# The second feed-forward layer of token block B as seven quarter products instead of eight, in a float32 decoder layer on one core

## The chip, the cores and the metric

One Trainium2 chip, one of its cores. The metric is the device time of one execution of the whole program in microseconds. Engines: TensorE (PE, with its weight loads as PEld), VectorE (DVE), ScalarE (ACT), GpSimd (POOL), SyncE (SP, which here only issues DMAs).

## What is computed

One hybrid decoder layer in float32: 1024 prompt tokens and 8 sample tokens, width 1024. Only its last third matters here:

```python
x = x + jnp.einsum('bte,ed->btd', mix, p['w_out'])        # 1024 x 1024
h2 = rmsnorm(x, p['norm_ffn_g'])
u = jnp.square(jax.nn.relu(jnp.einsum('btd,df->btf', h2, p['w_up'])))   # 1024 -> 4096
x = x + jnp.einsum('btf,fd->btd', u, p['w_down'])         # 4096 -> 1024
```

The outputs are the rows x of all tokens, and keys, values and recurrent states of the attention part, which comes earlier.

## The kernel before

**Numbers.** Each operand of a dense product is split in two parts of the type fp32r, a high one (a copy in that type, made by ScalarE) and a low one (value minus high, made by VectorE). A product of two tiles is three matmuls: high by high, high by low, low by high (`split_matmuls`, lines 85, 86 and 87, which serve all dense products). The stationary operand is a 128x128 piece of the weights, the moving one a piece of the tokens' data.

**Blocks.** The tokens are worked on in two blocks: A has prompt tokens 0 to 511, B has the other 512 and the 8 sample tokens, in two spans of 256 and 264 columns. The program goes through a front part (all tokens' projections), then `feed_forward` for A, with attention and recurrences of both blocks woven between its steps, then `feed_forward` for B with nothing beside it. Block B's part is what the change touches.

**Feed-forward of B.** The order on TensorE is: eight tiles "out" (`w_out`, 8 tiles x 2 spans x 24 matmuls), and then eight groups g. A group has four tiles "up" x = 0 to 3 (128 of the 4096 inner features each: 2 spans x 8 inputs x 3 = 48 matmuls a tile) and one "down" part: the group's 512 inner features into the 1024 outputs, that is 8 output tiles o x 2 spans x 4 inputs x 3 = 192 matmuls. Each of the 16 sums of a down part takes one PSUM bank in turn out of four, and VectorE adds it to the rows `xt` (line 2254). The output is kept transposed in `xt`, and at the end TensorE turns it tile by tile (`turn_y`, line 2045), ScalarE copies it (`copy_y`, line 2113) and SP stores it. Two of the four turns of prompt tokens stand inside the last down part, and there are two buffers `y`.

**Beside TensorE**, each engine has its instructions in an order written out by hand, and executes them in that order. In each up tile of B:

- ScalarE: high part of 128 rows of `w_down` (line 2095, 128x1024), high part of the up weights two tiles ahead (`split_high`, line 2080, 128x1024), for each span the square (line 2153) and the high part of the result (line 2155). It also issues the loads of `w_down` (line 2102).
- VectorE: low part of the `w_down` rows (line 2190, 128x1024), for each span relu and scaling out of PSUM (line 2236), low part of the up weights two tiles ahead (`split_low`, line 2084, 128x1024), for each span the low part of the squares (line 2243). In the down part it has the 16 adds.
- GpSimd: in the out tiles the sum of squares for the norm (line 2179), one `pow` for it (line 2184), and nothing in the groups.
- SP: loads of up weights, three tiles ahead.

Group 0 has the norm in it. TensorE sums the squares after tile 0 (line 1975), VectorE scales them (line 2195), GpSimd takes the root (line 2184), VectorE makes five small diagonal pieces (line 2200), and in the middle of tile 1's second span TensorE spreads these over the partitions (line 1982). ScalarE copies the result (line 2145), and only then can the first relu run.

What orders the engines are semaphores. `take` makes TensorE wait until the bank's former owner was read:

```python
    def take(pe, kind, *key):
        i = place[kind, key]
        if i >= BANKS:
            pe.wait_ge(*freed(i - BANKS))
```

Of the kernel before, what the change touches and what calls it, by code (L numbers as in the profile page):

```python
# [15 lines left out]
P = 128  # L16
# [3 lines left out]
NS = 8  # L20
# [60 lines left out]
def split_matmuls(pe, out, lhs, rhs, ks, first, last):  # L81

    for n, k in enumerate(ks):
        (lh, ll), (rh, rl) = lhs(k), rhs(k)
        pe.matmul(out, lh, rh, start=first and n == 0, stop=False)  # L85
        pe.matmul(out, lh, rl, start=False, stop=False)  # L86
        ins = pe.matmul(out, ll, rh, start=False, stop=last and n == len(ks) - 1)  # L87
    return ins
# [1678 lines left out]
def feed_forward(nc, a, m, ps, sem, at, part):  # L1767
    spans = [(0, HALF)] if part == 0 else [(0, 256), (256, 264)]
    NP = len(spans)
    N = HALF + part * NS  # L1770
    BANKS = 2 + 2 * part
    sfx = "AB"[part]
    mh, ml = m["mh"][part], m["ml"][part]
    xt, xr, rb2 = m["xt"], m["xr"], m["rb2"]
    x2h = at("x2h" + sfx, (59.5, 166.625)[part], [P, KT, NB], FP32R)
    x2l = at("x2l" + sfx, (75.75, 182.875)[part], [P, KT, NB], FP32R)
# [14 lines left out]
    if part:  # L1791
        norm_tiles.append((slice(N - P, N), slice(HALF, N)))
# [4 lines left out]


    OUT0, UP0, DOWN0 = KT * part, FT * FGROUPS * part, KT * FGROUPS * part

    def out_no(u, p):
        return OUT0 + NP * u + p

    def up_no(g, x, p):
        return UP0 + NP * (FT * g + x) + p

    def down_order(g):
        if part and g == FGROUPS - 1:
            return [(o, p) for p in range(NP) for o in range(KT)]
        return [(o, p) for o in range(KT) for p in range(NP)]  # L1810

    def down_no(g, o, p):
        return DOWN0 + NP * KT * g + down_order(g).index((o, p))


    order = [("out", (u, p)) for u in range(KT) for p in range(NP)]
    for g in range(FGROUPS):
        order += [("up", (g, x, p)) for x in range(FT) for p in range(NP)]
        order += [("down", (g, o, p)) for o, p in down_order(g)]
    place = {what: i for i, what in enumerate(order)}  # L1820

    def freed(i):
        kind, key = order[i]
        if kind == "out":
            return x2_made, out_no(*key) + 1
        if kind == "up":
            return v_made, up_no(*key) + 1
        return added, down_no(*key) + 1

    def norm_bank(p):  # L1830
        return 7 - p if part else 6
# [4 lines left out]
    def take(pe, kind, *key):  # L1836
# [3 lines left out]
        elif part == 0:  # L1840
            m["dense_bank_free"](pe, i)
        elif i < 2:
            pe.wait_ge(added, DOWN0)
        else:
            m["side_banks_free"](pe)

    def tile_no(t):
        return TILES * part + t

    def tile_done(t):  # L1850

        if t >= KT:
            g, x = divmod(t - KT, FT)
            return up_ready, up_no(g, x, NP - 1) + 1
        if t >= 0:
            return out_ready, out_no(t, NP - 1) + 1
        return up_ready, UP0 + t + 1

    def tokens(p):
        return slice(spans[p][0], spans[p][0] + spans[p][1])  # L1860

    ALL = slice(0, N)

    def sync(sp, beside):
        def load_up(t):
            if part or t >= 2:
                sp.wait_ge(up_low, tile_no(t) - 1)
            else:
                sp.wait_ge(sem("w_low"), 22 + t)
# [11 lines left out]
        def load_residual(u):  # L1881
            if u >= 2:
                sp.wait_ge(x2_made, out_no(u - 2, NP - 1) + 1)
            elif part:
                sp.wait_ge(u_low, UP0)
            else:
                m["residual_stored"](sp)
            sp.dma_start(xr[:, u % 2, 0:N], a["xt_scratch"].rearrange("p (k n) -> p k n", n=NT)
                         [:, u, part * HALF:part * HALF + N]).then_inc(xr_in[u % 2], 16)

        def store_y(t):

            n = 4 * part + t
            sp.wait_ge(y_copied, n + 1)
            if t == 4:
                sp.dma_start(a["y_sample"], m["y"][0:NS, t % 2, :]).then_inc(sem(f"y_out{t % 2}"), 16)
            else:
                sp.dma_start(a["y_prompt"][(4 * part + t) * P:(4 * part + t + 1) * P, :], m["y"][:, t % 2, :])\
                    .then_inc(sem(f"y_out{t % 2}"), 16)

        if part == 0:
            load_up(2)
        for t in range(KT):
            load_residual(t)
            load_up(t + 3)
            if t >= KT - 2 and part == 0:
                first_down(t - KT + 2)
            if part and t in (0, 2):
                m["store_yA"](t)
                m["store_yA"](t + 1)  # L1910
# [3 lines left out]
        for g in range(FGROUPS):  # L1914
            for x in range(FT):
                t = KT + FT * g + x
                if t + 3 < TILES or part == 0:
                    load_up(t + 3)
# [6 lines left out]
        m["store_y" + sfx] = store_y  # L1925
# [7 lines left out]
    def tensor(pe, beside):  # L1933
# [3 lines left out]
        def out_part(u, p, ks):  # L1937
            if ks[0] == 0:
                pe.wait_ge(up_low, tile_no(u) + 1)
                take(pe, "out", u, p)  # L1940
            ins = split_matmuls(pe, ps[:, bank("out", u, p), 0:spans[p][1]], weights(u),
                                lambda k: (mh[:, k, tokens(p)], ml[:, k, tokens(p)]), ks, ks[0] == 0, ks[-1] == KT - 1)
# [3 lines left out]
        def first_outs():  # L1946

            for i in range(2):
                pe.wait_ge(sem("mix_low"), 8 if i else 4)
                for u in range(2):  # L1950
                    out_part(u, 0, range(4 * i, 4 * i + 4))
                    beside(2 * i + u)

        def first_out():

            for p in range(NP):
# [1070 lines left out]
```

## Time and profile before

| | us |
|---|---|
| time, median of 3 runs | 1424.47 (1423.86 to 1426.74) |
| span of the profiled execution, first to last instruction | 1424.1 |
| TensorE busy | 1375.1 (97% of the span) |
| VectorE busy | 834.5 (59%) |
| ScalarE busy | 542.6 (38%) |
| GpSimd busy | 318.1 (22%) |
| start of B's first up tile | about 1041.5 |
| one group of B | 46.0 |
| last matmul of B's last down part | 1415.0 |

The profiled execution's span is its own time but for what lies outside its instructions. It stands 0.4 below the median of the runs and inside their range. Start times in all rows count from the first instruction of the span. "Busy" of an engine is the union of its instructions. In a timeline row "x2" means two instructions after each other shown as one, and "idle" names what ended the wait.

### The profile page before, as it was taken

The page shows a single profiled execution, that of the slowest core. Times are in us where ns is not written, and L with a number is a line of the kernel's source. Part 1 is how long each engine was busy: PE and PEld are TensorE (multiplying, and loading weights), DVE is VectorE, ACT ScalarE, POOL GpSimd, SP SyncE. Part 2 cuts the span into 40 slices and gives each one's busy share as a digit, 9 for nine tenths or more (in the row PEclk, how much of TensorE's full clock was granted, in tenths as well). Part 3 has the DMA queues.
Part 4 walks back from the last instruction along what each step waited for, and adds up shares of the span by engine and source line. Part 5 has one row for each costly group of instructions (what it writes and reads, how often), then busy time and mean ns, then how long its engine had stood idle before and what let it go on. Part 6 is the DMA issues. An engine that isn't in the chain of part 4 may idle for free.

```text
span 1424.1 us, 23612 instructions
## 1 busy us (share of the span) xinstructions
PE 1375.1 (97%) x8781; PEld 1145.8 (80%) x8781; DVE 834.5 (59%) x1416; ACT 542.6 (38%) x1011; POOL 318.1 (22%) x363
## 2 busy tenths in 40 slices
PE   7998999999999999998999999999999999999998
PEld 6767777776777767776767767667999999999998
DVE  5469667745648886758667564444454455445542
ACT  6444332414546554533325241332442234223431
POOL 2546624435523534342000000000220000000000
PEclk9999999999999999999999999999999999999999
DMA  8547745434255553453377565971532233123311
GB/s 273 147 129 236 219 131 169 140 120 140 89 159 168 184 174 112 132 165 121 104 240 240 190 218 174 315 245 62 179 125 76 90 119 104 60 75 119 119 31 60
DMA packets 115635, 211.99 MB, mean 149 GB/s; under 512 B 12665, under 2 KB 45722, under 8 KB 115522
## 3 DMA queue, kind: packets, MB, share of 16 engines
q1 hardware_dynamic: 104306, 176.94, 38.3%
q10 hardware_dynamic: 11216, 33.57, 7.4%
q8 instruction: 69, 1.13, 0.3%
q14 instruction: 44, 0.36, 0.1%
HBM read 184.00 MB, written 26.46 MB: 148 GB/s over the span
## 4 chain that ended last, share of the span: by engine, by line
PE 64%; DVE 5%; ACT 3%; issue 2%; DMA 0%; ACTq 0%; POOL 0%; SPq 0%; DVEq 0%; POOLq 0%
PE ps L85 18%; PE ps L87 17%; PE ps L86 17%; PE ps L2634 2%; PE ps L1495 2%; PE ps L1532 2%; PE ps L1314 1%; DVE uw_l L2084 1%; PE ps L1516 1%; ACT uw_h L2080 1%; DVE ul L2243 1%; PE ps L1728 1%; DVE sd L2388 1%; DVE dl L2190 1%; DVE xr L2236 0%
## 5 line engine op out<-in xcount | busy, mean ns | idle before, releaser
L85 PE MATMUL ps<-uh,dh 128*128 128x512 f32 (+2 forms) x768 | 250.0, 326 | 5.0 <-DVE dl L2190 3.9
L87 PE MATMUL ps<-uh,dl 128*128 128x512 f32 (+2 forms) x768 | 245.4, 320 | 0.0
L86 PE MATMUL ps<-ul,dh 128*128 128x512 f32 (+2 forms) x768 | 245.0, 319 | 0.0
L2399 POOL TENSOR_TENSOR kr<-kr,qb 128x512 f32<-128x512 f32 x128 | 175.9, 1385 | 167.4 <-DMA kr<-in_cache_k 167.0
L2254 DVE TENSOR_TENSOR xt<-xt,ps 128x256 f32<-128x256 f32 (+2 forms) x192 | 97.6, 512 | 164.6 <-PE ps L87 164.1
L85 PEld LDWEIGHTS ps<-uh,dh 128*128 128x128 f32 x768 | 144.4, 188 | 25.3 <-DVE xt L2254 7.6
L87 PEld LDWEIGHTS ps<-uh,dl 128*128 128x128 f32 x768 | 144.5, 188 | 11.5
L86 PEld LDWEIGHTS ps<-ul,dh 128*128 128x128 f32 x768 | 144.6, 188 | 9.7
L2095 ACT ACTIVATE dh<-raw_dn 128x1024 fp32r<-128x1024 f32 x64 | 67.5, 1055 | 215.6 <-PE ps L87 214.9
L2080 ACT ACTIVATE uw_h<-raw_up 128x1024 fp32r<-128x1024 f32 x80 | 84.5, 1056 | 163.4 <-PE ps L87 163.3
L85 PE MATMUL ps<-x2hB,uw_h 128*128 128x264 f32 (+1 forms) x512 | 145.2, 284 | 0.7 <-DVE x2lB L2218 0.7
L86 PE MATMUL ps<-x2lB,uw_h 128*128 128x264 f32 (+1 forms) x512 | 144.7, 283 | 0.0
L87 PE MATMUL ps<-x2hB,uw_l 128*128 128x264 f32 (+1 forms) x512 | 144.5, 282 | 0.0
L2084 DVE TENSOR_TENSOR uw_l<-raw_up,uw_h 128x1024 fp32r<-128x1024 f32 x80 | 99.7, 1246 | 35.6 <-ACT uw_h L2080 35.5
L85 PE MATMUL ps<-x2hA,uw_h 128*128 128x512 f32 x256 | 106.4, 416 | 0.0
L2388 DVE TENSOR_REDUCE sd<-kr 128x8 f32<-128x512 f32 x128 | 84.9, 675 | 33.2 <-POOL kr L2399 33.1
L87 PE MATMUL ps<-x2hA,uw_l 128*128 128x512 f32 x256 | 101.9, 398 | 0.0
L86 PE MATMUL ps<-x2lA,uw_h 128*128 128x512 f32 x256 | 101.6, 397 | 0.0
L2190 DVE TENSOR_TENSOR dl<-raw_dn,dh 128x1024 fp32r<-128x1024 f32 x64 | 81.0, 1266 | 28.2 <-ACT dh L2095 24.3
L85 PEld LDWEIGHTS ps<-x2hB,uw_h 128*128 128x128 f32 x512 | 96.5, 189 | 0.9 <-DVE x2lB L2218 0.9
L2236 DVE SCALAR_TENSOR_TENSOR xr<-ps,rb 128x256 f32<-128x256 f32 (+1 forms) x96 | 49.0, 514 | 81.1 <-PE ps L87 76.9
L86 PEld LDWEIGHTS ps<-x2lB,uw_h 128*128 128x128 f32 x512 | 96.5, 188 | 0.0
(339 smaller groups left out, 2840.0 us busy)
## 6 DMA issues: line engine op xcount, KB each, us to landing
kr<-in_cache_k SPq DMA_DIRECT2D x128, 256.0 KB, 3.1
raw_up<-in_w_up_units SPq DMA_DIRECT2D x64, 512.0 KB, 4.7
vr<-in_cache_v SPq DMA_DIRECT2D x128, 256.0 KB, 3.5
raw_dn<-in_w_down ACTq DMA_DIRECT2D x62, 512.0 KB, 3.6
raw<-in_w_in_units SPq DMA_DIRECT2D x23, 512.0 KB, 5.1
raw_up<-in_w_out_units SPq DMA_DIRECT2D x16, 512.0 KB, 4.4
xin<-in_x_prompt SPq DMA_DIRECT2D x8, 512.0 KB, 5.4
xt_scratch<-xts SPq DMA_DIRECT2D x8, 512.0 KB, 5.9
```

What stands on the lines that cost most here:

```text
L85: pe.matmul(out, lh, rh, start=first and n == 0, stop=False)
L86: pe.matmul(out, lh, rl, start=False, stop=False)
L87: ins = pe.matmul(out, ll, rh, start=False, stop=last and n == len(ks) - 1)
L1495: pe.matmul(ps[:, score_bank(n, c) + j // 512, 0:x], qt[r, b, i * P:(i + 1) * P], kt[r, b, j:j + x], start=True, stop=j + x < w)
L2080: act.activation(uw_h[:, t % 2, :, :], raw_up[:, t % 2, :].rearrange("p (k c) -> p k c", c=P), ACT.Copy).then_inc(up_high, 1)
L2084: dve.tensor_tensor(uw_l[:, t % 2, :, :], raw_up[:, t % 2, :].rearrange("p (k c) -> p k c", c=P), uw_h[:, t % 2, :, :].bitcast(FP32), ALU. ...
L2095: act.activation(dh[:, x, :], raw_dn[:, x % 2, :], ACT.Copy).then_inc(dn_high, 1)
L2190: dve.tensor_tensor(dl[:, x, :], raw_dn[:, x % 2, :], dh[:, x, :].bitcast(FP32), ALU.subtract).then_inc(dn_low, 1)
L2236: dve.scalar_tensor_tensor(vt[:, i % 2, 0:spans[p][1]], ps[:, bank("up", g, x, p), 0:spans[p][1]], 0.0, rb2[:, tokens(p)], ALU.max, ALU.mu ...
L2254: dve.tensor_tensor(xt[:, o, c], xt[:, o, c], ps[:, bank("down", g, o, p), 0:spans[p][1]], ALU.add).then_inc(added, 1)
L2388: dve.tensor_reduce(m["sd"][:, b, g, :], place(v)[:, :].rearrange("p (h d) -> p h d", d=DH), X, ALU.add).then_inc(k_used, 1)
L2399: pool.tensor_tensor(k[:, :], k[:, :], qb[v // PAGES][:, :], ALU.mult).then_inc(k_multiplied, 1)
```

## The change

`feed_forward` is cut in two functions. `feed_first` is its code for block A, with the same instructions in the same order. `feed_last` is block B's, and its out tiles, its norm and its up products are as before. New is the down part. For a group, the 512x1024 weights are taken as 2 x 2 quarters A11, A12, A21, A22 of 256x512 (two 128-row tiles k by four output tiles j), and the squares u as 2 x 2 quarters U11, U12, U21, U22 (inner tiles 0, 1 or 2, 3; span 0 or 1, of which span 0 is padded with 8 zero columns). Then:

```python
FACTORS = ["A11", "A12", "S1", "S3", "S2", "A22", "S4"]
PRODUCTS = {"P1": ("A11", "U11", "X"), "P2": ("A12", "U21", "Y"), "P3": ("S4", "U22", "Z"), "P4": ("A22", "T4", "X"),
            "P5": ("S1", "T1", "Z"), "P6": ("S2", "T2", "X"), "P7": ("S3", "T3", "X")}
BEGINS = ("P1", "P5", "P2")
AFTER = {"P6": "P1", "P7": "P6", "P4": "P7", "P3": "P5"}

def products(g):
    if g == FGROUPS - 1:
        return [(x, j) for x in ("P1", "P6", "P2", "P7", "P5", "P4", "P3") for j in range(PAIRS)]
    return ([("P1", j) for j in range(PAIRS)]
            + [(x, j) for js in ((0, 1), (2, 3)) for x in ("P5", "P6", "P2", "P7", "P3", "P4") for j in js])
```

Each of the 28 pieces (x, j) of a group is 2 inputs x 3 = 6 matmuls (P2 and P4 of 256 columns, the others of 264), 168 in all. P6, P7 and P4 go on in the bank that P1 began, P3 in the bank that P5 began, and VectorE adds the bank to `xt` after each piece, so each piece goes to another tile and span of the rows. A piece that goes on in a bank waits for the add before it:

```python
        def product(g, x, j):
            name, part, kind = PRODUCTS[x]
            if x in BEGINS:
                take(pe, "down", (g, x, j))
            else:
                pe.wait_ge(added, added_no(g, AFTER[x], j))
            if j == 0:
                pe.wait_ge(dn_low, factor_no(g, name))
            ...
```

GpSimd makes the sums of weights, four instructions of 128x1024 a group, all between SBUF tensors:

```python
            pool.tensor_tensor(s1[:, :, :], a21, a22, ALU.add).then_inc(sq_added, 1)
            pool.tensor_tensor(a21, a11, a21, ALU.subtract).then_inc(sq_added, 1)
            pool.wait_ge(dn_low, factor_no(g, "A11"))
            pool.wait_ge(sq_added, sum_no(g, "S3"))
            pool.tensor_tensor(a11, s1[:, :, :], a11, ALU.subtract).then_inc(sq_added, 1)
            pool.wait_ge(dn_low, factor_no(g, "A12"))
            pool.wait_ge(sq_added, sum_no(g, "S2"))
            pool.tensor_tensor(a12, a12, a11, ALU.subtract).then_inc(sq_added, 1)
```

On GpSimd the first group's S1 and S3 stand right behind the norm's `pow`. Each of the seven factors has a high part on ScalarE and a low part on VectorE (128x1024 each). The four differences of the squares, T1 to T4, are made by VectorE (`change`, two each, 128x264 or 128x256), and the seven parts U11, T1, T2, U21, T3, U22, T4 have a high and a low part (two each). VectorE's order in one group:

```python
            low_factor(g, "A11")
            low_factor(g, "A12")
            relu(g, 0, 0)
            relu(g, 0, 1)
            low_part(g, "U11", 0)
            change(g, "T1", 0)
            if g:
                split_low(dve, t + 2)
            low_part(g, "T1", 0)
            low_factor(g, "S1")
            low_factor(g, "S3")
            relu(g, 1, 0)
            relu(g, 1, 1)
            low_part(g, "U11", 1)
            change(g, "T1", 1)
            split_low(dve, t + 3)
            low_part(g, "T1", 1)
            low_factor(g, "S2")
            relu(g, 2, 0)
            relu(g, 2, 1)
            low_part(g, "U21", 0)
            change(g, "T2", 0)
            change(g, "T3", 0)
            if more:
                split_low(dve, t + 4)
            low_part(g, "U22", 0)
            change(g, "T4", 0)
            low_part(g, "T2", 0)
            low_part(g, "T3", 0)
            low_part(g, "T4", 0)
            low_factor(g, "A22")
            relu(g, 3, 0)
            relu(g, 3, 1)
            low_part(g, "U21", 1)
            change(g, "T2", 1)
            change(g, "T3", 1)
            low_part(g, "T2", 1)
            change(g, "T4", 1)
            low_part(g, "T3", 1)
            low_part(g, "U22", 1)
            low_part(g, "T4", 1)
            low_factor(g, "S4")
            todo = products(g)
            for what in todo[:6]:
                add(g, *what)
            if more:
                split_low(dve, t + 5)
            for what in todo[6:]:
                add(g, *what)
```

ScalarE's order follows it: `split_high` of a later tile stands between the square of span 1 and the high parts of the T's; each high part waits for the square or the difference that it copies, each high factor for the last use of its buffer in the group before. The loads of `w_down` move from ScalarE's queue to SP's: those of group g + 1 are issued in two pairs, when S4 and the low part of S2 of group g are made, and when the low part of its S4 is. The last group's output has a buffer of its own for each tile: one turn stands inside the down part, four behind it, ScalarE copies three of the five and VectorE two.

## Rows read from the trace of the kernel before

**Rows 1.** The page: busy time, share of the span, instructions of each engine.

```profile
PE 1375.1 (97%) x8781; PEld 1145.8 (80%) x8781; DVE 834.5 (59%) x1416; ACT 542.6 (38%) x1011; POOL 318.1 (22%) x363
```

**Rows 2.** Windows (stretch: length, busy us (count) per engine, PEclk, DMA): one up, one down part.

```profile
1137.31:1160.32 23.01, 23.01 (x194) 23.01 (x193) 13.94 (x21) 12.01 (x20) 0.00 (x0) 1.00 0.36 123
1160.32:1183.33 23.01, 23.01 (x195) 23.01 (x194) 8.71 (x19) 2.43 (x5) 0.00 (x0) 1.00 0.18 62
```

**Rows 3.** Groups by line and form, 1060 to 1400: count, busy us, mean ns, idle before.

```profile
L2190 DVE TENSOR_TENSOR dl<-raw_dn,dh 128x1024 fp32r<-128x1024 f32 x30 | 36.8, 1226 | 20.0 <-ACT dh L2095 20.0
L2095 ACT ACTIVATE dh<-raw_dn 128x1024 fp32r<-128x1024 f32 x30 | 31.8, 1059 | 145.7 <-PE ps L87 145.0 <-issue 0.3
L2254 DVE TENSOR_TENSOR xt<-xt,ps 128x264 f32<-128x264 f32 x56 | 24.0, 428 | 50.6 <-PE ps L87 50.6
```

**Rows 4.** Timeline of DVE (start, us, instruction): instructions behind each other.

```profile
1065.50 0.76 DVE L2243 TENSOR_TENSOR ul<-xr,uh 128x256 fp32r<-128x256 f32 x2
1152.75 1.23 DVE L2190 TENSOR_TENSOR dl<-raw_dn,dh 128x1024 fp32r<-128x1024 f32 x1 [0.64 <-ACT dh L2095]
1153.89 0.42 DVE L2236 SCALAR_TENSOR_TENSOR xr<-ps,rb 128x256 f32<-128x256 f32 x1
```

**Rows 5.** Timeline, block A: DVE and POOL where both work between SBUF tensors.

```profile
643.33 1.23 DVE L2190 TENSOR_TENSOR dl<-raw_dn,dh 128x1024 fp32r<-128x1024 f32 x1 [3.75 <-ACT st_new L2687]
643.43 2.28 POOL L2399 TENSOR_TENSOR kr<-kr,qb 128x512 f32<-128x512 f32 x1 [8.10 <-DMA kr<-in_cache_k]
644.47 0.68 DVE L2236 SCALAR_TENSOR_TENSOR xr<-ps,rb 128x512 f32<-128x512 f32 x1
645.07 1.72 DVE L2084 TENSOR_TENSOR uw_l<-raw_up,uw_h 128x1024 fp32r<-128x1024 f32 x1
645.67 2.27 POOL L2399 TENSOR_TENSOR kr<-kr,qb 128x512 f32<-128x512 f32 x1
646.72 1.78 DVE L2243 TENSOR_TENSOR ul<-xr,uh 128x512 fp32r<-128x512 f32 x1
```

**Rows 6.** POOL: one line's durations (min/median/max), and the group of its smallest two-input operation.

```profile
L2399 POOL TENSOR_TENSOR kr<-kr,qb x128: 1259/1293/2323, 91.3 to 660.9; 128x512 f32<-128x512 f32 x128
...
L1611 POOL TENSOR_TENSOR oss<-oss,stat 128x1 f32<-128x1 f32 x32 | 6.2, 193 | 37.5 <-ACT ps L1571 35.0
```

**Rows 7.** Timeline of group 0: the norm, its spread, the first relu.

```profile
1048.12 1.17 PE L1975 MATMUL ps<-ones,acc 128*128 128x1 f32 x10
1049.58 2.16 POOL L2184 TENSOR_TENSOR norm<-norm,half 128x5 f32<-128x5 f32 x1 [3.69 <-DVE norm L2195]
1051.77 1.02 DVE L2200 TENSOR_SCALAR norm<-ident,norm 128x128 f32<-128x128 f32 x5 [1.07 <-POOL norm L2184]
1053.16 1.04 PE L1982 MATMUL ps<-norm,ones 128*128 128x256 f32 x4
```

**Rows 8.** Timeline of the end.

```profile
1415.03 0.28 PE L87 MATMUL ps<-uh,dl 128*128 128x264 f32 x1
1415.83 1.97 PE L2045 MATMUL ps<-ident,xt 128*128 128x128 f32 x16 [0.52 <-DVE xt L2254]
1416.96 1.94 ACT L2113 ACTIVATE y<-ps 128x1024 f32<-128x1024 f32 x2 [6.35 <-PE ps L2045]
1420.68 1.01 ACT L2113 ACTIVATE y<-ps 8x1024 f32<-8x1024 f32 x1 [1.78 <-DMA out_y_prompt<-y]
```

**Rows 9.** Windows at two waits of TensorE in the attention part, and behind them (columns as rows 2).

```profile
134.20:137.30 3.10, 0.33 (x2) 0.00 (x0) 3.06 (x8) 0.00 (x0) 1.35 (x2) 1.00 0.69 186
138.30:141.50 3.20, 3.20 (x17) 3.20 (x17) 3.13 (x6) 0.00 (x0) 1.07 (x2) 0.50 1.03 310
273.20:275.80 2.60, 0.29 (x2) 0.00 (x0) 2.60 (x4) 0.93 (x1) 0.00 (x0) 1.00 0.50 126
275.90:279.30 3.40, 3.40 (x18) 2.65 (x20) 3.30 (x6) 0.37 (x1) 0.03 (x1) 1.00 0.55 188
```

**Rows 10.** The page: DMA issues (count, KB each, us from issue to landing).

```profile
raw_dn<-in_w_down ACTq DMA_DIRECT2D x62, 512.0 KB, 3.6
```

More of the change, by code:

```diff
@@ L1796, in feed_forward, with up_no, down_no @@
     y_turned, y_copied = sem("y_turned"), sem("y_copied")
[L1799 to L1816, printed above, removed]
+    def up_no(g, x):
+        return FT * g + x
+    def down_no(g, o):
+        return KT * g + o
+    order = [("out", (u,)) for u in range(KT)]
     for g in range(FGROUPS):
-        order += [("up", (g, x, p)) for x in range(FT) for p in range(NP)]
-        order += [("down", (g, o, p)) for o, p in down_order(g)]
+        order += [("up", (g, x)) for x in range(FT)]
+        order += [("down", (g, o)) for o in range(KT)]
     place = {what: i for i, what in enumerate(order)}
@@ L1924, in sync @@
                 tick += 1
[L1925 removed]
+        m["store_yA"] = store_y
     def preload(sp):
@@ L1986, in up @@
             t = KT + FT * g + x
[L1987 to L2001 removed]
+            pe.wait_ge(up_low, t + 1)
@@ new lines, in up @@
+            take(pe, "up", g, x)
+            for i in range(2):
+                for k in range(i * KT // 2, (i + 1) * KT // 2):
+                    if g == 0 and x == 0:
+                        pe.wait_ge(x2_low, k + 1)
+                    ins = split_matmuls(pe, ps[:, bank("up", g, x), :], weights(t),
+                                        lambda k: (x2h[:, k, ALL], x2l[:, k, ALL]), [k], k == 0, k == KT - 1)
+                    if g == 0 and x == 1 and k == 4:
+                        spread()
+                if i:
+                    ins.then_inc(up_ready, 1)
+                beside(tick + i)
@@ L2054, in tensor @@
+        first_outs()
+        for u in range(2, KT):
             out(u)
@@ L2063, in tensor @@
             tick += KT
-        if part:
-            for t in range(2, 5):
-                turn_y(t)
     def before_tile(u, beside):
@@ L2245, in vector @@
                 beside(tick + 2 * x + 1)
-                if x + 1 == FT and more:
+                if x + 1 == FT:
                     split_low(dve, t + 2)
-            for i, (o, p) in enumerate(down_order(g)):
-                if part == 0 or i % NP == 0:
-                    beside(tick + 2 * FT + i // NP)
-                c = tokens(p)
-                n = down_no(g, o, p)
-                dve.wait_ge(down_ready, n + 1)
-                dve.tensor_tensor(xt[:, o, c], xt[:, o, c], ps[:, bank("down", g, o, p), 0:spans[p][1]], ALU.add).then_inc(added, 1)
+            for o in range(KT):
+                beside(tick + 2 * FT + o)
+                dve.wait_ge(down_ready, down_no(g, o) + 1)
+                dve.tensor_tensor(xt[:, o, ALL], xt[:, o, ALL], ps[:, bank("down", g, o), :], ALU.add).then_inc(added, 1)
```

789 lines of the change are left out of this document (569 added, 220 removed).

## The prediction

> **What bounds the kernel now.** The page's busy times come first: TensorE is busy for 97% of the span, every other engine for under 60% [rows 1]. The reader is to see that TensorE is the bound as an average, no more. The windows of one group of B show how it is there: 23.01 of 23.01 us busy in the up part and again in the down part, VectorE busy 13.9 and 8.7 [rows 2]. So a group takes 46.02 us, all of it matmuls, 192 in 23.01 us, 0.1198 us each. A matmul less is 0.12 us less, for as long as no engine feeding TensorE comes too late. VectorE has 23.4 us of slack in a group; whether the new work fits, and in which order, is the question. Everything before B's first group keeps its instructions, so I cost it at nothing.
>
> **What is removed.** 24 matmuls in each of 8 groups: 24 x 0.12 = 2.9 us a group, 23.0 us in all. If TensorE never waited, a group would take 43.1 us.
>
> **What is added, by engine.**
>
> VectorE in a group: 11 instructions of 128x1024 (seven factors, four up weights; it had 8) and 58 small ones (8 relus, 8 differences, 14 low parts, 28 adds; it had 32). The large form shows 1.23 us [rows 3], but the next instruction starts 1.14 after it, and small ones follow each other at 0.34 (two of 0.42 make 0.76) [rows 4]; I take 0.35, since most have 264 columns. That is 12.5 + 20.3 = 32.8 us of work, under 43. It would fit if it were not in one order.
>
> ScalarE: 11 large at 1.06 [rows 3] and 22 small of about 0.42, 21 us. Not a bound, but VectorE waits for it inside a group.
>
> GpSimd: four instructions of 128x1024. None is in the trace. The nearest is 128x512, undisturbed 1.29 (the median); the floor is one of these and the ceiling two (2.6). With one element it is 0.19, so 1.1 us is for 511 elements and 1024 come to 2.4 [rows 6]. I take 2.4.
>
> The loads of `w_down` go to SP, which has nothing else urgent. They take 3.6 us to land [rows 10]. The first pair is issued in tile 2's share of the group, the second ahead of the adds, 15 us or more before the next group's first use. Hidden; with that cover gone TensorE would wait for what exceeds it.
>
> **The locked pair.** GpSimd and VectorE don't work side by side when both have two SBUF inputs. At 643.43 GpSimd's `kr` waits for `dl` and takes 2.28 in place of 1.29; `uw_l` starts at 645.07 and runs 1.72 instead of 1.23, until 1.1 after the end of `kr`; the next `kr` waits in turn (2.27), and the next `ul` takes 1.78 [rows 5]. They alternate, whole instruction by whole instruction. The relu out of PSUM between them takes its usual 0.68. In the new order factors, differences and low parts are of the locked kind; relus and adds are not.
>
> **The stretch that sets a group.** VectorE executes in order, so its first add stands behind everything else of the group, and piece P6 can't start until P1's bank was added. From the relu of tile 0's second span (0.2 after TensorE ends that tile) to the first add VectorE has 8 large and 29 small instructions: 9.1 + 10.15 = 19.3 us. To it come waits:
> - S2 and S4 start when the low part of A12 ends, 2.8 us into the group, and end at 7.6; the low part of U11 is due at 6.3: 1.4 us blocked.
> - After the relus of tiles 1, 2 and 3 the low part waits for a square and a copy on ScalarE: 0.42 x 3 with 0.1 of signals, less the 0.7 of VectorE's own two relus, 0.7 each: 2.1.
> - ScalarE's `split_high` (1.06) stands ahead of T1's copy: 0.6. Four smaller ones of this kind: 0.6.
>
> Sum 24.0, and with the add's own 0.43: 24.4, or 24.6 after tile 0. TensorE needs for three tiles, the four pieces P1 and two P5 144 + 24 + 12 = 180 matmuls, 21.6 us. **It waits 3.0 us for P6**, and 0.4 more at P7, since after six adds VectorE makes a large low part. The other 22 pieces take 15.8. A group is 5.75 + 24.6 + 0.4 + 15.8 = 46.5 us, against 46.02: the gain of 2.9 is eaten by a wait of 3.4.
>
> **Group 0** is worse. GpSimd's S1 and S3 stand right behind `pow`, which ends at 1051.7, and the five norm pieces (tensor_scalar out of SBUF) start there [rows 7]. Whether these are locked rows 5 don't say. They had no GpSimd work beside them, so 0 is the low end; alternating they lose 2 x 2.4 = 4.8. I take the latter, as most of VectorE's SBUF work behaves so. TensorE stands at the spread since 1053.1 and gets it at 1057.4: 4.3 us. Then up tile 3 needs its low weights. VectorE from 1057.3: A11, A12 to 1059.6, two relus, U11 blocked by S2 to 1062.4, T1 blocked by S4 to 1065.1, its low part (with 0.6 of wait) to 1066.0, S1 and S3 (0.6 of wait) to 1068.9, relus, U11, T1 (0.7 of wait) to 1071.0, 0.6 of wait and the weights to 1072.9. TensorE is there at 1065.6: 7.3 us. Then P6 and P7 4.4. Against it stand 2.9 of matmuls and 0.8 of a wait for `dl` that the old group 0 had. Net +12.3.
>
> **The end.** Two turns took 1.97 [rows 8]. The old last group held two, 48.0 us; the new one holds one and, with each product's four pieces in a row, no P7 wait: 46.5 - 0.4 + 1.0 = 47.1. That is -0.9. Behind the last matmul at 1415.03 the program takes 9.1 us: turns, copies, a wait for a buffer of `y` from 1417.97 (ScalarE's copies of 1.0 end) to 1420.68, a small copy and store [rows 8]. With five buffers no copy waits. Four turns of 1.0 end 4.1 after the last matmul; VectorE's copy of tile 3 (1.2, like its other large ones) starts at 3.1 and ends at 4.3, and a store takes some 3 more (the wait for one above was 2.7): 7.5. I take -1.5, between 0 (stores collide) and -2.7.
>
> **Sum** with TensorE's clock as it is: +12.3 + 6 x 0.5 - 0.9 - 1.5 = +12.9, 1424.1 + 12.9 = 1437.0.
>
> **The clock.** After a wait of 3.1 us at 134.2 TensorE ran at 1.2 GHz (0.50) for the 3.2 us shown, after one of a good 2.6 at 273.2 it stayed at 2.4 [rows 9]. The new kernel has ten waits of 3 us or more, near the first of these. A stretch of 3.4 at half rate loses 1.7 us of matmuls. I charge six of the ten: 10 us. **Forecast 1447 us.** The profiled span stands 0.4 under the median of runs; that is inside the rounding.
>
> The Trainium skill ("TensorE: Matmul & The Clock Gate", "Why this matters for your kernels") says that idle gaps between bursts of matmuls put the clock back. It speaks against this change: by it every one of the ten waits could cost, by the shorter row of the trace none.
>
> **Rivals.** 0.2% (2.9 us) is about what a measurement of this kernel tells from no change.
> - *TensorE keeps setting the pace (faster).* Its place is the wait for P6: if VectorE's stretch is 3 us shorter (small instructions at 0.31, say, and ScalarE's results earlier), it vanishes. Then -23 - 1.5, and group 0 gives back 5 to 15: 1405 to 1415. For it: VectorE has 10 us of slack in the sum. Against: in-order execution, and the rows' 0.34. Up to half of the wait left gives up to 1421. Chance 0.13.
> - *The lock costs nothing.* GpSimd's work falls into VectorE's waits; 1.4 less a group and 9 less in group 0: 1424 to 1427 with the clock kept. Against: rows 5. Chance 0.10, half of it within 0.2%.
> - *The clock stays up (slower, less).* All as forecast without the 10 us: 1430 to 1440. For it: the wait of 2.6. Chance 0.22.
> - *The forecast*, 1440 to 1456. Chance 0.42.
> - *VectorE's stretch is longer (slower, more).* New instructions have two waits on semaphores, and rows of this kind are few. At 0.40 a small one, 29 x 0.05 is 1.5 us a group, 12 us in all, and all waits trip the clock: 1456 to 1470. Chance 0.13.
> - *It does not save matmuls*: 168 against 192 stand in the code; no chance.
>
> **Numbers.** Faster 0.13, same 0.05, slower 0.82. The range leaves out most of the first case and the upper part of the last: 1421 to 1463.
>
> **What would show it.** The down part of a middle group has 168 matmuls and a single wait at P6 of about 3 us, released by the add; VectorE is without idle time ahead of it but for waits on ScalarE; the period is 46.5 (48 where the clock fell); up tile 3 of group 0 waits about 7 us for `uw_l`; the norm pieces and low parts beside GpSimd take 2.4 longer. PEclk shows 0.5 behind most P6 waits. A period near 43 with no wait at P6 would show the VectorE account wrong; a wait at P6 of 1 or 2 us the sizes.

## The result, and the profile after

The changed kernel takes 1439.94 us (median of 4 runs, 1438.91 to 1445.23) against 1425.56 for the kernel before on the same chip (4 runs, 1423.86 to 1426.74): a ratio of 1.0104, interval 1.0081 to 1.0126, **slower by 14 us**. The prediction said 1447 with 1421 to 1463 around it. The profiled execution was the longest of the four: 1445.23, span 1443.5.

The page of the changed kernel, as [rows 1] of before:

```profile
PE 1371.0 (95%) x8589; PEld 1137.6 (79%) x8589; DVE 949.2 (66%) x1651; ACT 576.1 (40%) x1081; POOL 402.5 (28%) x395
```

192 matmuls are gone (8781 to 8589), but TensorE's busy time fell by 4.1 us only and the span grew by 19.4. Windows of the changed kernel by group say where. The first is group 0, the third group 2, the fourth group 3, the last group 7; then the up part and the down part of group 3, as [rows 2]. After the length stand busy us (count) of PE, PEld, DVE, ACT and POOL, then PEclk, DMA share, GB/s.

```profile
1044.43:1105.21 60.78, 49.46 (x376) 48.30 (x375) 45.05 (x78) 23.62 (x40) 19.13 (x8) 0.94 0.23 79
1105.21:1152.85 47.64, 45.08 (x362) 44.86 (x361) 36.27 (x69) 18.87 (x33) 10.49 (x4) 0.96 0.26 89
1152.85:1200.18 47.33, 45.09 (x363) 44.88 (x361) 35.87 (x69) 18.88 (x33) 10.45 (x4) 0.96 0.26 90
1200.18:1246.25 46.07, 43.83 (x362) 43.42 (x361) 35.78 (x69) 18.87 (x33) 10.46 (x4) 1.00 0.26 92
...
1388.25:1434.93 46.68, 44.36 (x370) 44.14 (x368) 34.06 (x67) 15.63 (x30) 5.71 (x2) 1.00 0.00 1
...
1200.18:1223.19 23.01, 23.01 (x194) 23.01 (x193) 18.37 (x30) 13.06 (x23) 5.71 (x2) 1.00 0.17 56
1223.19:1246.25 23.06, 20.82 (x170) 20.41 (x169) 17.41 (x40) 5.80 (x11) 4.75 (x2) 1.00 0.35 128
```

The reader is to see three things. The up part is what it was, 23.01 of 23.01. The down part takes 23.06 although it has 24 matmuls fewer: 2.24 us of it TensorE idles. And the groups come in two lengths: 46.07 with the clock at 1.00, 47.33 with 0.96 (groups 2, 4, 5 and 6); group 3 alone has the first length, and group 1 takes 47.64. Against 46.02 before (49.83 in group 0, 47.62 in the last) that is +10.95 in group 0, +6.9 over the six in the middle, -0.9 in the last. With -0.5 behind the last matmul, block B costs 16.4 us more. The 3.0 us that are left of the 19.4 lie ahead of B, where the instructions are the same. B's first up tile starts at 1044.43 in this profile, 1041.46 in that of before, and between 1038.5 and 1043.8 in those of the experiments that leave the part ahead of it alone. The same instructions vary by that much from profile to profile, so I don't put the 3.0 down to the change. The lower clock alone doesn't order them: the experiment that starts B at 1042.20 has a mean PEclk of 1.00 up to 1038, the one that starts it at 1038.54 has 0.99.

The waits by line over block B, changed kernel (waiting instruction, releaser: us in total, times, longest):

```profile
PE ps L85 <- DVE xt L2680: 18.2, 8, 2.6
...
DVE part_l L2671 <- ACT part_h L2523: 15.0, 26, 0.6
...
PE ps L85 <- DVE uw_l L2495: 4.8, 1, 4.8
...
PE ps L2423 <- DVE norm L2642: 3.7, 1, 3.7
```

So one large wait a group, eight times, for VectorE's adds (L2680), and the two in group 0 that were forecast: up tile 3 for its low weights, the spread for the norm pieces (the five small diagonal pieces that it is made with). Before, TensorE had no such wait in a middle group [rows 2]. The one at P6 of group 3, TensorE's timeline:

```profile
1227.47 0.28 PE L87 MATMUL ps<-part_h,fl 128*128 128x264 f32 x1
1229.99 0.39 PE L85 MATMUL ps<-part_h,fh 128*128 128x264 f32 x1 [2.23 <-DVE xt L2680]
```

2.52 from start to start, 2.4 of it lost. And VectorE's order ahead of that add, same group:

```profile
1206.11 0.43 DVE L2650 SCALAR_TENSOR_TENSOR u<-ps,rb 128x264 f32<-128x264 f32 x1 [2.47 <-PE ps L87]
1206.46 1.70 DVE L2671 TENSOR_TENSOR part_l<-u,part_h 128x264 fp32r<-128x264 f32 x1
...
1213.58 0.43 DVE L2671 TENSOR_TENSOR part_l<-u,part_h 128x264 fp32r<-128x264 f32 x1 [0.60 <-ACT part_h L2523]
...
1227.36 1.10 DVE L2671 TENSOR_TENSOR part_l<-u,part_h 128x264 fp32r<-128x264 f32 x3
1228.38 1.22 DVE L2633 TENSOR_TENSOR fl<-raw_dn,fh 128x1024 fp32r<-128x1024 f32 x1
1229.52 2.09 DVE L2680 TENSOR_TENSOR xt<-xt,ps 128x256 f32<-128x256 f32 x6
1231.52 1.22 DVE L2495 TENSOR_TENSOR uw_l<-raw_up,uw_h 128x1024 fp32r<-128x1024 f32 x1
```

The bank of the first P1 piece is full before 1225, and its add starts at 1229.52, since the low parts of the T's and then S4's low factor (L2633, 1.22) stand ahead of it. From the relu of the second span to the add it is 23.4 us. The bracket at 1213.58 is one of the waits for ScalarE that the sum held; the 1.70 at 1206.46 is a low part blocked beside GpSimd, as in [rows 5] ("the block" from here on). GpSimd's side of it:

```profile
1202.02 3.31 POOL L2609 TENSOR_TENSOR raw_dn<-s,raw_dn 128x1024 f32<-128x1024 f32 x1 [10.22 <-DVE fl L2633]
1205.47 2.39 POOL L2612 TENSOR_TENSOR raw_dn<-raw_dn,raw_dn 128x1024 f32<-128x1024 f32 x1
```

S4 ends at 1207.86, and the low part of 0.43 us ends 0.3 later. The relu at 1206.11, with one input out of PSUM, ran beside it in its usual 0.43. S2 in turn was held up by the large low factor that VectorE had started.

Group 0 (VectorE's timeline, then GpSimd's), the counterpart of [rows 7]:

```profile
1054.74 5.23 DVE L2642 TENSOR_SCALAR norm<-ident,norm 128x128 f32<-128x128 f32 x5 [1.07 <-POOL norm L2624]
...
1063.66 1.26 DVE L2671 TENSOR_TENSOR part_l<-u,part_h 128x264 fp32r<-128x264 f32 x1 [0.60 <-ACT part_h L2523]
1064.85 2.63 DVE L2667 TENSOR_TENSOR t<-u 128x264 f32<-128x264 f32 x1
...
1073.81 1.23 DVE L2495 TENSOR_TENSOR uw_l<-raw_up,uw_h 128x1024 fp32r<-128x1024 f32 x1 [0.48 <-ACT uw_h L2491]
```

```profile
1054.68 2.38 POOL L2605 TENSOR_TENSOR s<-raw_dn,raw_dn 128x1024 f32<-128x1024 f32 x1
1057.02 2.34 POOL L2606 TENSOR_TENSOR raw_dn<-raw_dn 128x1024 f32<-128x1024 f32 x1
1061.33 3.30 POOL L2609 TENSOR_TENSOR raw_dn<-s,raw_dn 128x1024 f32<-128x1024 f32 x1 [1.98 <-DVE fl L2633]
```

The five norm pieces take 5.23 us where they took 1.02 [rows 7]: they begin with S1 and end right behind S3. That was the open question of the prediction's group 0, and the answer is that a tensor_scalar from SBUF to SBUF is blocked too. The Trainium skill ("SBUF — State Buffer", "Who interferes with whom") counts tensor_scalar among VectorE's operations that can take the port pair shared with GpSimd; the trace agrees, 5.23 beside GpSimd's two sums against 1.02.

The clock, windows of 3.4 us behind two waits that are alike (2.52 both), as [rows 9]:

```profile
1184.10:1187.40 3.30, 3.30 (x18) 3.30 (x17) 2.59 (x6) 0.00 (x0) 0.34 (x1) 0.50 0.92 331
1230.00:1233.40 3.40, 3.40 (x26) 3.20 (x27) 3.40 (x9) 0.00 (x0) 0.00 (x0) 1.00 0.79 287
```

Behind the first TensorE ran at 1.2 GHz (0.50), behind the second at 2.4. In B there are seven such stretches of 3.4 us at ten waits; the one at tile 3 of group 0 begins 0.3 before the wait ends, the others 0.1 to 1.4 after. Those of group 0 cost no time. From 1054.8 to the group's first add at 1088.48 VectorE waits 5.1 us in all, for ScalarE and GpSimd, and never for TensorE: it alone sets the pace there, and a slower TensorE only waits less afterwards.

The end, the counterpart of [rows 8]: timeline, then windows.

```profile
1434.93 0.29 PE L87 MATMUL ps<-part_h,fl 128*128 128x264 f32 x1
...
1437.87 1.23 DVE L2686 COPY yB<-ps 128x1024 f32<-128x1024 f32 x1 [0.52 <-PE ps L2471]
1438.74 1.01 ACT L2528 ACTIVATE ys<-ps 8x1024 f32<-8x1024 f32 x1 [0.72 <-PE ps L2471]
```

```profile
1438.50:1440.00 1.50, 0.21 (x2) 0.00 (x0) 0.60 (x1) 1.01 (x1) 0.00 (x0) 1.00 1.03 421
1440.00:1441.50 1.50, 0.00 (x0) 0.00 (x0) 0.00 (x0) 0.00 (x0) 0.00 (x0) 1.00 1.02 418
```

No copy waits for a buffer now, but the DMA engines are full (share 1.03 and 1.02) when every other engine has finished: four stores of 512 KB leave behind the last matmul instead of two. From 1434.93 to 1443.5 it is 8.6 us, against 9.1.

### The profile page after: what moved, and what is told of

The parts are those of the page before. It is cut to its first block, busy times and chain, and to the rows that moved or that the text cites. A ratio compares the mean times of both kernels' runs of the same rounds, so it can differ in the third digit from the quotient of the medians.

```text
span 1443.5 us, 23824 instructions
## 1 busy us (share of the span) xinstructions
PE 1371.0 (95%) x8589; PEld 1137.6 (79%) x8589; DVE 949.2 (66%) x1651; ACT 576.1 (40%) x1081; POOL 402.5 (28%) x395
## 4 chain that ended last, share of the span: by engine, by line
PE 51%; DVE 14%; ACT 6%; issue 4%; POOL 1%; DMA 0%; ACTq 0%; DVEq 0%; SPq 0%; POOLq 0%
PE ps L85 14%; PE ps L87 13%; PE ps L86 13%; DVE part_l L2671 3%; DVE fl L2633 3%; PE ps L3141 2%; DVE uw_l L2495 2%; PE ps L1532 2%; PE ps L1495 2%; ACT u L2515 1%; PE ps L1314 1%; ACT uw_h L2491 1%; DVE uw_l L2002 1%; DVE u L2650 1%; ACT uw_h L1998 1%
## 5 line engine op out<-in xcount | busy, mean ns | idle before, releaser
L85 PE MATMUL ps<-part_h,fh 128*128 128x264 f32 (+1 forms) x448 | 131.5, 294 | 18.2 <-DVE xt L2680 18.2
L86 PE MATMUL ps<-part_l,fh 128*128 128x264 f32 (+1 forms) x448 | 130.5, 291 | 0.0
L87 PE MATMUL ps<-part_h,fl 128*128 128x264 f32 (+1 forms) x448 | 130.5, 291 | 0.0
L2680 DVE TENSOR_TENSOR xt<-xt,ps 128x264 f32<-128x264 f32 (+1 forms) x224 | 90.8, 424 | 49.0 <-PE ps L87 48.7
L85 PE MATMUL ps<-uh,dh 128*128 128x512 f32 x256 | 105.0, 410 | 3.6 <-DVE dl L2088 2.6
L85 PEld LDWEIGHTS ps<-part_h,fh 128*128 128x128 f32 x448 | 88.1, 197 | 20.3 <-DVE xt L2680 20.3
L87 PE MATMUL ps<-uh,dl 128*128 128x512 f32 x256 | 100.9, 394 | 0.0
L86 PE MATMUL ps<-ul,dh 128*128 128x512 f32 x256 | 100.5, 393 | 0.0
L87 PEld LDWEIGHTS ps<-x2hB,uw_l 128*128 128x128 f32 x512 | 97.7, 191 | 0.0
L87 PEld LDWEIGHTS ps<-part_h,fl 128*128 128x128 f32 x448 | 88.0, 196 | 0.0
```

Source lines behind the costliest of these rows:

```text
L85: pe.matmul(out, lh, rh, start=first and n == 0, stop=False, skip_group_check=onto)
L86: pe.matmul(out, lh, rl, start=False, stop=False, skip_group_check=onto)
L2680: dve.tensor_tensor(xt[:, o, c], xt[:, o, c], ps[:, down_bank(g, PRODUCTS[x][2], j), 0:c.stop - c.start], ALU.add)\
```

## The experiments

The theory: VectorE has time enough in a group (35.8 of 46.07 us busy) but does its work in the wrong order. What stands ahead of the first add is paid by TensorE; what stands behind it is not. The rivals: VectorE's load as such, GpSimd's block in the steady groups, or the order of TensorE's own pieces. The ratios of the experiments are to the kernel before, timed on the same chip as each of them.

**Large low factors behind adds.** S4's and A22's low parts move behind eight and ten adds, the weights behind fourteen; ScalarE's and SP's orders follow.

```diff
-FACTORS = ["A11", "A12", "S1", "S3", "S2", "A22", "S4"]
+FACTORS = ["A11", "A12", "S1", "S3", "S2", "S4", "A22"]
...
-            low_factor(g, "A22")
             relu(g, 3, 0)
...
-            low_factor(g, "S4")
             todo = products(g)
-            for what in todo[:6]:
-                add(g, *what)
-            if more:
-                split_low(dve, t + 5)
-            for what in todo[6:]:
+            for n, what in enumerate(todo):
+                if n == 8:
+                    low_factor(g, "S4")
+                if n == 10:
+                    low_factor(g, "A22")
+                if n == 14 and more:
+                    split_low(dve, t + 5)
                 add(g, *what)
```

> The low parts of S4 and A22 (1.14 us each) go from ahead of the first add to behind the eighth and the tenth add, the low part of the next up weights behind the fourteenth; the work is the same. Theory (VectorE's order of work ahead of the first add sets a group): the stretch is 2.3 us shorter, the wait for P6 (2.4 us in the changed kernel's trace) falls to under 0.5, no clock falls there, a middle group takes 43.5 to 44.5 us and the whole 1412 to 1422 us. Rival (VectorE has too much work in a group, wherever it stands): the group stays at 46 to 47.3 and the whole at 1436 to 1441. Rival (the chain of pieces in one bank costs the wait): the same, no change at P6.

Measured: 1418.48 us (1414.88 to 1420.16), ratio to before 0.9941 (0.9921 to 0.9960). The same instructions in another order turn a kernel 1% slower into one 0.6% faster. A middle group of this kernel (windows), VectorE's timeline in it, and TensorE's wait for adds from 1105 to 1380:

```profile
1193.25:1236.77 43.52, 43.52 (x363) 43.34 (x362) 35.25 (x69) 18.99 (x33) 10.47 (x5) 1.00 0.27 98
```

```profile
1216.33 1.11 DVE L2671 TENSOR_TENSOR part_l<-u,part_h 128x264 fp32r<-128x264 f32 x3
1217.35 2.77 DVE L2680 TENSOR_TENSOR xt<-xt,ps 128x256 f32<-128x256 f32 x8
1220.03 1.22 DVE L2633 TENSOR_TENSOR fl<-raw_dn,fh 128x1024 fp32r<-128x1024 f32 x1
```

```profile
PE ps L85 <- DVE xt L2680: 0.3, 1, 0.3
```

43.52 of 43.52 us busy, with VectorE's work unchanged (busy 35.25 us against 35.78) and GpSimd's block still in place. What is left of the wait is under 0.3 us: at P6 two matmuls start 0.25 and 0.23 us after the one before them, where 0.12 is usual. Group, wait and total are in the ranges of the theory. Group 0 hardly moved (59.08 against 60.78). Its waits for the spread and for tile 3 are as they were (4.0 and 5.2 us from start to start).

**P2's pieces ahead of P6's.** TensorE's own order, to give VectorE two more pieces of time.

```diff
-            + [(x, j) for js in ((0, 1), (2, 3)) for x in ("P5", "P6", "P2", "P7", "P3", "P4") for j in js])
+            + [(x, j) for js in ((0, 1), (2, 3)) for x in ("P5", "P2", "P6", "P7", "P3", "P4") for j in js])
```

> In all groups but the last, TensorE (and VectorE's adds with it) takes the pieces P2 between P5 and P6. If the bank that P6 shares with P1 made the wait, 1.4 us of other work in it would shorten each group by 1.4 us and more, to 1425 to 1430 in all. By the theory of VectorE's order the adds are as late as ever: the wait at P6 falls by 1.4 but one of 2 or more us appears at P7, whose bank waits for the add of P6, which now stands behind P2's adds and the split of the up weights. Group 46 to 47, the whole 1433 to 1442, with fewer stretches at 1.2 GHz, as no single wait is much over 2 us.

Measured: 1446.22 us, ratio 1.0147 (1.0125 to 1.0169), slower than the change itself. Middle groups take 46.8 or 48.3 (group 1: 48.6). VectorE's timeline, and TensorE's waits from 1100 to 1400, which is groups 1 to 6:

```profile
1225.58 2.09 DVE L2680 TENSOR_TENSOR xt<-xt,ps 128x256 f32<-128x256 f32 x6
1227.58 1.22 DVE L2495 TENSOR_TENSOR uw_l<-raw_up,uw_h 128x1024 fp32r<-128x1024 f32 x1
1228.72 1.43 DVE L2680 TENSOR_TENSOR xt<-xt,ps 128x256 f32<-128x256 f32 x4
```

```profile
PE ps L85 <- DVE xt L2680: 17.7, 12, 2.1
```

The one wait became two (12 in six groups): at P6 for what was left, 1.1 to 1.4 us, and at P7 for 2.4, since behind six adds still stand the low up weights (1.22) and P2's adds, which now come ahead of P6's. The bank that P7 needs is emptied later. The wait that VectorE's order causes was not removed by giving TensorE other work first; it moved to the next bank. The second wait was forecast; the total was not (1433 to 1442), and 1425 to 1430, the rival's, is further off.

**First sums early (group 0).** S1 and S3 of group 0 are made between the last additions of squares, ahead of the norm.

```diff
+            if v == KT - 3:
+                summed(0)
+            if v == KT - 2:
+                second()
...
         for g in range(FGROUPS):
-            summed(g)
+            if g:
+                summed(g)
+                second()
+            rest(g)
```

> GpSimd makes the first group's S1 and S3 between the sums of squares of the out tiles, ahead of the norm's root, instead of behind it. Theory (the five norm pieces of VectorE alternate with these two sums, 2.4 us each): the wait at the spread, 4.0 us, goes; the wait of up tile 3 for its low weights (5.1 us) stays at 4 to 6, since S2 and S4 still stand against the low parts there. Group 0 shorter by 3.5 to 5 us plus a stretch at 1.2 GHz, the whole 1433 to 1437. Rival (the norm pieces were late for another reason, such as the pow): no change.

Measured: 1438.5 us (1433.56 to 1441.47), ratio 1.0072 (1.0048 to 1.0096). Group 0 takes 56.58, 4.2 less. The norm pieces are back at their old 1.02:

```profile
1053.71 1.02 DVE L2654 TENSOR_SCALAR norm<-ident,norm 128x128 f32<-128x128 f32 x5 [1.07 <-POOL norm L2633]
```

So GpSimd's two sums were what held them, and the whole of VectorE's order up to the first add comes 4.2 us sooner. Tile 3's wait grew from 5.1 to 6.4: TensorE arrives there 5.5 us sooner, VectorE 4.2. The total shows less. It missed its range (1433 to 1437) by 1.5, and its interval overlaps the change's (1.0081 to 1.0126); in the profile 1.2 of the 4.2 us are lost again in group 1 (48.88 for 47.64), at a longer stretch of the lower clock.

**S2 and S4 of one column.** GpSimd's two later sums are cut to one column of each 128x1024 block, which leaves the rest of them out of the computation: the block in the steady groups is taken away.

```diff
-            pool.tensor_tensor(a11, s1[:, :, :], a11, ALU.subtract).then_inc(sq_added, 1)
+            pool.tensor_tensor(a11[:, :, 0:1], s1[:, :, 0:1], a11[:, :, 0:1], ALU.subtract).then_inc(sq_added, 1)
...
-            pool.tensor_tensor(a12, a12, a11, ALU.subtract).then_inc(sq_added, 1)
+            pool.tensor_tensor(a12[:, :, 0:1], a12[:, :, 0:1], a11[:, :, 0:1], ALU.subtract).then_inc(sq_added, 1)
```

> Leaves out the sums S2 and S4 but for one column of each row tile (the factors hold A11 and A12 there), in all groups. Theory: the low part of U11 runs in 0.43 us instead of 1.70, VectorE's stretch is 1.3 us shorter, the wait for P6 falls from 2.4 to 1.1 to 1.7 (part of what is won is spent waiting for ScalarE), fewer or no stretches at 1.2 GHz; in group 0 the wait for the low weights falls by 2 to 4 us. Group 45 to 45.5 and the whole 1424 to 1430. Rival (GpSimd's sums fall into VectorE's own waits): middle groups unchanged at 46.1 without and 47.3 with a stretch at 1.2 GHz.

Measured: 1435.24 us (1433.47 to 1436.89), ratio 1.0070 (1.0047 to 1.0093). P6's wait is 2.04 in every middle group in place of 2.52, and the groups take 45.6 or 46.8. VectorE's timeline, the place of the 1.70 above:

```profile
1198.03 0.42 DVE L2671 TENSOR_TENSOR part_l<-u,part_h 128x264 fp32r<-128x264 f32 x1
...
1199.55 1.23 DVE L2495 TENSOR_TENSOR uw_l<-raw_up,uw_h 128x1024 fp32r<-128x1024 f32 x1 [0.51 <-ACT uw_h L2491]
```

The low part is 1.3 us shorter, but 0.2 is lost ahead of T1's difference and 0.6 at the low up weights, which now wait for ScalarE's `split_high`. From there to the first add every instruction is 0.5 sooner, and that is what reaches TensorE. The block is real and was a fifth of the wait. More was forecast (a wait of 1.1 to 1.7, 1424 to 1430 in all), and the total's interval overlaps the change's, so the finding rests on the groups. In group 0 VectorE's first add comes 2.4 us sooner, yet the group takes 60.79: tile 3's wait fell from 5.1 to 1.9, P6's rose from 2.4 to 3.7, and 6.8 us at the lower clock lie around its end (PEclk 0.89 against 0.94).

**Both moves.** The first and the third together.

> The moved factors of the first experiment (1418.5 us) and the early first sums of the third together. Theory: the two act in different places and add up: middle groups 43.5 us, group 0 some 4 us shorter than the 59.1 of the first experiment (the wait at the spread goes, the one for tile 3's low weights grows by about 1), the whole 1412 to 1417. Rival (what group 0 wins at the spread it gives back at tile 3): 1417 to 1419.

Measured: 1413.20 us (1411.43 to 1414.11), ratio 0.9902 (0.9885 to 0.9918). Groups: 54.58, 43.85, then 43.52 or 43.53. Group 0 is 4.5 us shorter than in the first experiment, and the total is in the range forecast, under the rival's. The ratios of the medians add up too, from the change's 1.0104: -0.0163 and -0.0032 make 0.9909, though the second is within the noise. What is left is group 0's wait at tile 3, 6.4 us.

**Four factors ahead of the norm.** With both moves, the low and high factors A11, A12, S1 and S3 of group 0 are made ahead of the norm, in VectorE's idle time there; GpSimd holds S2 and S4 back until the norm pieces are done.

```diff
+            low_factor(g, "A11")
+            low_factor(g, "A12")
             if g == 0:
+                low_factor(g, "S1")
+                low_factor(g, "S3")
                 norm()
...
-            low_factor(g, "A11")
-            low_factor(g, "A12")
...
+            else:
+                pool.wait_ge(norm_scaled, 4)
             rest(g)
```

> As the one before, and in group 0 the high and low parts of A11, A12, S1 and S3 (low: 4 x 1.14 us on VectorE) stand ahead of the norm's steps, in 4.6 us in which VectorE has nothing to do; the sums S2 and S4 wait until the norm pieces are made. Theory (group 0 is VectorE's in-order work between the norm and tile 3's low weights): the wait for these weights, 6.3 us in the third experiment, falls by 4 or more, the whole is 1407 to 1413. Rival (GpSimd's S2 and S4, 2.4 us each, hold the low parts of the squares whatever stands before): it falls by under 2 us, 1412 to 1416.

Measured: **1407.94 us** (1406.79 to 1409.31), ratio 0.9872 (0.9855 to 0.9888), faster than both kernels: 18 us under before. The page, then group 0, a middle group and the last one:

```profile
PE 1355.5 (96%) x8589; PEld 1124.9 (80%) x8589; DVE 937.6 (67%) x1651; ACT 577.8 (41%) x1081; POOL 402.0 (29%) x395
```

```profile
1039.68:1089.86 50.18, 46.35 (x376) 45.40 (x375) 39.30 (x78) 23.76 (x40) 14.29 (x7) 1.00 0.27 95
...
1133.72:1177.27 43.55, 43.55 (x363) 43.36 (x361) 35.25 (x69) 19.01 (x33) 10.46 (x4) 1.00 0.27 98
...
1351.39:1396.87 45.48, 44.35 (x370) 44.13 (x368) 33.51 (x67) 15.74 (x30) 5.72 (x3) 1.00 0.01 1
```

Group 0 fell to 50.18, near the 49.83 of before. Its waits are 0.9, 1.9 and 1.5 us from start to start now (tile 3's was 6.4), the longest in B is 1.9, and the clock stands at 1.00 in all of B. Total and wait are as the theory had them. VectorE is busy for 67% of the span, in the changed kernel for 66%, and 18 of the 23.0 us that removing 192 matmuls was to save are earned at last.

**More work, behind the adds and ahead of them.** The first of a pair of kernels puts one more 128x1024 operation on VectorE (a maximum of U's first two tiles with themselves, which changes nothing) behind the twentieth add; the second makes S4's low factor twice, ahead of the first add.

```diff
+            again = u[:, 0:2, :, 0:256]
+            dve.tensor_tensor(again, again, again, ALU.max)
+            for what in todo[20:]:
```

> The changed kernel with one more VectorE instruction of 128x1024 in each group, behind the twentieth of the 28 adds (a maximum of the squares with themselves, whose result nobody uses). Theory (position decides): adds behind it are 1.2 us late once and catch up by 0.3 us each, no wait of TensorE is longer by more than 0.5; the whole within 2 us a group at most, 1439 to 1444. Rival (amount decides): +1.1 us in each of 8 groups, 1448 to 1450.

```diff
+            dve.wait_ge(dn_high, factor_no(g, "S4"))
+            m["dve_steps"].then(dve.tensor_tensor(factor(fl, "S4"), factor_source("S4"), factor(fh, "S4").bitcast(FP32),
+                                                  ALU.subtract))
             low_factor(g, "S4")
```

> The changed kernel with the low part of S4 made twice in each group, ahead of the first add (128x1024, the second copy overwrites the first with the same values; it also waits for the first to end, about 0.1 us). Theory: the wait for P6 grows by 1.2 to 1.3 us in every group, to 3.7, and now every one of them is followed by a stretch at 1.2 GHz: group 47.3 + 1.25 = 48.6, the whole 1449 to 1453. Rival (the amount of VectorE's work decides): the same as with the extra instruction behind the adds.

Behind: 1443.44 us (1443.01 to 1444.78), ratio 1.0121 (1.0104 to 1.0138); its interval overlaps the change's 1.0081 to 1.0126. Groups 2 to 6 take 46.08 or 47.34, as without it, and P6's wait there is 2.52 to 2.54; the total is in the range of position, not of amount (1448 to 1450). Ahead: 1460.79 us (1458.06 to 1463.66), ratio 1.0240 (1.0218 to 1.0262). VectorE's timeline of the second, and its waits from 1100 to 1430:

```profile
1231.98 1.22 DVE L2754 TENSOR_TENSOR fl<-raw_dn,fh 128x1024 fp32r<-128x1024 f32 x1
1233.24 1.23 DVE L2633 TENSOR_TENSOR fl<-raw_dn,fh 128x1024 fp32r<-128x1024 f32 x1
1234.38 2.09 DVE L2680 TENSOR_TENSOR xt<-xt,ps 128x256 f32<-128x256 f32 x6
```

```profile
PE ps L85 <- DVE xt L2680: 24.9, 7, 3.8
```

The same 1.2 us of VectorE work cost nothing that is clear of the noise at one place and 1.26 at P6 at the other (2.52 to 3.78). This settles it between load and order. The total rose by more than eight times that, by some 20 us, and missed its range (1449 to 1453): the lower clock now came with all eight P6 waits, and lasted 6.8 us in place of 3.4 at four of them, where it began 1.0 to 1.5 before the wait ended.

The kernel with the work behind the adds also shows what the lower clock costs in group 0. It is the changed kernel up to there, but TensorE kept 2.4 GHz behind the spread. It reached tile 3 sooner and waited 6.6 us in place of 5.1, and the group still takes what it took in the changed kernel, 60.80 against 60.78 (windows):

```profile
1040.76:1101.56 60.80, 48.16 (x376) 47.01 (x375) 45.93 (x79) 23.64 (x40) 19.16 (x8) 0.94 0.23 79
```

## Why the prediction was right

**The direction and its cause hold.** The forecast case, a wait of TensorE for the add behind VectorE's in-order stretch, is what the trace shows, at the place named. The first experiment takes it away by order alone (the period is 43.52), and the last pair moves it with one instruction. The rivals: that TensorE keeps setting the pace fell (it does with the order of the first experiment); that the lock costs nothing fell (5.23 against 1.02; P6 2.52 against 2.04); that VectorE's stretch is longer fell (23.4, not over 24.0). The clock did not stay up, yet the median of 1439.94 lies at the upper edge of that rival's range, and 0.06 under the forecast case's own. So the total can't tell these two apart, and only the profile does. The range given for the lock rival, 1424 to 1427, does not follow from its terms: 1437.0 less seven times 1.4 and less 9 is 1418.

**Term by term**, forecast and measured, with the clock's part kept apart as there (47.33 - 46.07 = 1.26 for a stretch in a middle group, none for the two in group 0):

| term | forecast | measured |
|---|---|---|
| first relu to first add | 24.0 | 23.4 |
| wait at P6 | 3.0 | 2.4 |
| at P7, behind the large low part | 0.4 | 0.3 |
| middle group, clock kept | 46.5 | 46.07 |
| group 0 | +12.3 | +10.95 |
| last group | -0.9 | -0.9 |
| behind the last matmul | -1.5 | -0.5 |
| clock | +10 | 5 x 1.26 = 6.3 |

The six middle groups came to +0.3 with the clock kept and +0.3 more for group 1's slightly longer wait (47.64), where the sum had +3.0. B's sum is +16.4 where +22.9 was forecast: the clock was 3.7 too high, the middle groups 2.4, group 0 1.4, and the end 1.0 too low. 3.0 of the difference came back ahead of B in the profiled execution, so 1443.5 stood against 1447; that is luck, as the prediction had put that part at nothing.

- *P6.* The stretch was 0.6 us shorter than the sum of its rows. The prices of single instructions held (1.14 and 0.35 from start to start; GpSimd's 128x1024 2.39 against 2.4). The eight small waits for ScalarE were put at 3.3 and came to 3.0, the block at 1.4 and came to 1.3, which is also what the prediction's own times make (7.6 - 6.3), and the instructions were 0.1 shorter. The fourth experiment shows besides that such waits don't add: with the block gone, 0.8 of its 1.3 came back as waits for ScalarE.
- *The group without waits* was put at 43.1 and is 43.52. Some 0.1 of it is width: 120 of the new 168 matmuls have 264 columns and 48 have 256, where before they were half and half. A matmul of 264 takes 0.122 from start to start, one of 256 takes 0.118. The other 0.2 are the two late starts at P6 that the first experiment leaves.
- *Group 0.* The spread waited 3.9 (forecast 4.3), and tile 3 waited 5.0 (7.3). With the clock kept behind the spread, as in the kernel with work behind the adds, it is 6.5, and that is the number to set against 7.3. VectorE was 0.8 sooner than in the sum: 0.3 at the norm pieces, 0.3 where T1 and the low part of U11 were blocked, the rest in waits for ScalarE. P6 and P7 there cost 2.5. The 4.4 that the prediction gives for them has no working; with what the second stretch took from TensorE in between (14 matmuls 0.1 later each) they would come to some 3.9, an estimate.
- *The clock.* Six waits were charged with 1.7 each. Seven had a stretch at 1.2 GHz, and five of these cost 1.26. In such a group 16 matmuls start 0.22 us apart in place of 0.12, which is 1.6, and TensorE no longer waits the 0.3 at P7, as the adds catch up meanwhile. That group 0's stretches would be free, since VectorE sets the pace there, the sum had not seen.
- *The end.* The sum took a lone store's 3 us behind the last copy. The bound that it named against that, stores that collide, is what the trace points to: the DMA engines are full until 1441.5, with four stores of prompt tokens behind the last matmul. No run tests it.

What stays open: why the lower clock followed one wait of 2.52 us and not another of 2.52, and why the part ahead of B varies by some 6 us between profiles of the same instructions.

## What to carry to other kernels

When a change takes work from the engine that bounds and gives it to one with slack, make the sum over the stretch of the in-order queue that ends in the instruction others wait for, not over the whole period: 35.8 us of work in a group of 46 left 10 us idle, and with two large instructions ahead of the first add, and a third close behind it, a possible gain of 0.6% was still a loss of 1%. Put what frees a bank first and what only the next product needs behind it, and do the first group's extra work in the idle time ahead of a serial step such as the norm. Before GpSimd is given a long operation, look for what VectorE does between SBUF tensors beside it, the short and urgent ones above all. And count a stretch at the lower clock only where TensorE sets the pace.

## What the runs showed of the hardware

- A tensor_scalar of 128x128 from SBUF to SBUF is blocked by GpSimd's tensor_tensor: five took 5.23 us beside two sums and 1.02 without them. A relu out of PSUM beside the same operation kept its 0.43.
- TensorE's clock fell to 1.2 GHz for 3.4 us behind five of eight P6 waits of 2.4 to 2.8 us from start to start (all but those of groups 0, 3 and 7), and at eight of eight of 3.5 to 4.1, with 6.8 us at four of those. With S2 and S4 of one column it followed three of six waits of 2.04. In the fastest kernel no wait in B was over 1.9 and the clock never fell there. The Trainium skill ("TensorE: Matmul & The Clock Gate", "Why this matters for your kernels") warns of idle gaps between bursts; the traces agree that such gaps can bring the lower clock, and show, as [rows 9] had, that waits alike can end either way.
- So a wait's price was not proportional: 1.26 us more at each P6 made the kernel 20 us longer, twice the 8 x 1.26 = 10.1 of the waits themselves. And a stretch at the lower clock cost 1.26 where TensorE went on without a long wait, and nothing in group 0 (60.78 and 60.80 with different ones), where VectorE set the pace.
